# Last two experts added by TensorE, a reworked router chain, and the turns of silu rows between the halves of gate and up, in a one-core transformer layer

## The reference, cut to what matters

```python
h = rms_norm(x, g_attn);  z = h @ w_in            # q, k, v, indexer and gates
o_a, o_b = moba_attention(...), dsa_attention(...)
x = x + (sigmoid(ga) * (o_a @ w_br_a) + sigmoid(gb) * (o_b @ w_br_b)) @ w_out
x = x + hier_moe(rms_norm(x, g_ffn), ...)         # 4 groups of 8 experts
gate = sigmoid(rms_norm(x, g_ple) @ w_ple_gate)
x = x + gate * (p @ w_ple_proj)
return rms_norm(x, g_final)
```

## Time and profile before

| | us |
|---|---|
| median of 3 runs | 1038.18 (1036.38 to 1038.47) |
| the profiled execution | 1035.44 |
| its span | 1033.7 |
| TensorE matmul busy | 957.4 (93%) |
| VectorE, ScalarE, GpSimd busy | 369.2, 306.7, 146.7 |
| expert 0's first product begins | 479.2 |
| last down product ends | 951.1 |
| first turn of a tail tile begins | 965.6 |
| last gate products end | 1023.7 |

### The profile page before, as it was taken

One profiled execution on the slowest core, in us unless ns is written; L12 is line 12 of the kernel. 1 busy time (PEld: TensorE's weight loads), 2 busy tenths in 40 slices (PEclk: granted clock), 3 DMA queues, 4 the chain that ended last, 5 costly groups with the idle time before them and its releaser, 6 DMA issues.

```text
span 1033.7 us, 11751 instructions
## 1 busy us (share of the span) xinstructions
PE 957.4 (93%) x4688; PEld 587.7 (57%) x4688; DVE 369.2 (36%) x760; ACT 306.7 (30%) x527; POOL 146.7 (14%) x143
## 2 busy tenths in 40 slices
PE   5999999999999999987999999999999999997496
PEld 4776787576688888874434444444344334432374
DVE  4325696755453437236121111111011111031764
ACT  6334434746433124142111111111111111212464
POOL 0202123926600000020000000000000000001300
PEclk8999999999999999998999999999999999999698
DMA  9422131000072340846899999999999999999401
GB/s 313 145 82 82 41 114 16 1 2 1 2 285 82 114 171 3 323 158 273 348 420 421 421 421 420 420 421 420 421 422 420 421 421 415 421 420 382 165 21 61
DMA packets 58375, 256.03 MB, mean 248 GB/s; under 512 B 12094, under 2 KB 12734, under 8 KB 33232
## 3 DMA queue, kind: packets, MB, share of 16 engines
q1 hardware_dynamic: 49456, 248.26, 59.9%
q0 software_dynamic: 2560, 4.20, 1.1%
q10 hardware_dynamic: 6304, 2.80, 1.0%
HBM read 248.95 MB, written 10.49 MB: 251 GB/s over the span
## 4 chain that ended last, share of the span: by engine, by line
PE 85%; DVE 5%; DMA 4%; ACT 2%; POOL 2%; issue 1%; SPq 0%; ACTq 0%; POOLq 0%; DVEq 0%
PE psum L678 36%; PE psum L1003 11%; PE psum L1019 10%; PE psum L1004 9%; PE psum L965 6%; DMA slot<-in_w_up 3%; PE psum L984 2%; PE psum L974 2%; PE psum L1037 1%; DVE ht L1773 1%; PE psum L863 1%; PE psum L848 1%; PE psum L836 1%; PE psum L824 1%; DVE ple_gate_lo L1754 1%
## 5 line engine op out<-in xcount | busy, mean ns | idle before, releaser
L1003 PE MATMUL psum<-slot,xt 128*64 128x512 f32 x512 | 226.0, 594 | 2.2 <-DMA slot<-in_w_up 1.6
L1004 PE MATMUL psum<-slot,xt 128*64 128x512 f32 x512 | 226.1, 594 | 0.0
L1019 PE MATMUL psum<-slot,ht 128*64 128x512 f32 x256 | 116.7, 599 | 16.6 <-DVE ht L1773 16.6
L1773 DVE COPY ht<-psum 128x256 f32<-128x256 f32 x32 | 13.6, 425 | 330.7 <-PE psum L984 330.7
L678 PE MATMUL psum<-w_hi,act_hi 128*128 128x512 f32 x288 | 115.2, 400 | 6.1 <-DVE w_lo L544 6.1
L1020 PE MATMUL psum<-slot,ht 128*64 128x512 f32 x256 | 116.7, 598 | 0.0
L678 PE MATMUL psum<-w_lo,act_hi 128*128 128x512 f32 x288 | 112.9, 392 | 0.0
L678 PE MATMUL psum<-w_hi,act_lo 128*128 128x512 f32 x288 | 112.5, 391 | 0.0
L1003 PEld LDWEIGHTS psum<-slot,xt 128*64 128x64 f32 x512 | 68.5, 137 | 77.3 <-issue 75.4
L1004 PEld LDWEIGHTS psum<-slot,xt 128*64 128x64 f32 x512 | 68.5, 137 | 63.5 <-issue 63.4
L544 DVE TENSOR_TENSOR w_lo<-raw,w_hi 128x2048 fp32r<-128x2048 f32 (+1 forms) x31 | 70.5, 2274 | 83.9 <-ACT w_hi L539 83.8
(11 more groups left out here) (266 smaller groups left out, 1413.6 us busy)
## 6 DMA issues: line engine op xcount, KB each, us to landing
slot<-in_w_gate SPq DMA_DIRECT2D x64, 1024.0 KB, 19.0
slot<-in_w_up SPq DMA_DIRECT2D x64, 1024.0 KB, 19.9
slot<-in_w_down SPq DMA_DIRECT2D x64, 1024.0 KB, 20.9
raw<-in_w_in SPq DMA_DIRECT2D x22, 1024.0 KB, 5.0
raw<-in_w_out SPq DMA_DIRECT2D x4, 1024.0 KB, 5.2
slot<-in_w_ple_gate SPq DMA_DIRECT2D x4, 1024.0 KB, 20.9
pair_in<-pair_rows SPq DMA_DIRECT2D x4, 1024.0 KB, 8.3
rows_tok<-in_x SPq DMA_DIRECT2D x4, 512.0 KB, 6.7
```

The source lines that it names most:

```text
L1003: mm_g = pe.matmul(ps[FIRST:2 * FIRST, :], left, g[:, k, :], start=first, stop=last)
L1004: mm_u = pe.matmul(ps[0:FIRST, :], left, u[:, k, :], start=first, stop=last)
L1019: pe.matmul(ps[0:FIRST, :], left, w[:, k, 0:512], start=first, stop=last)
L1773: dve.tensor_copy(ht, h_turns(FIRST)).then_inc(ht_done, 1)
```

## The change

- Router: GpSimd's part of `x1_lo` goes to VectorE (`low_x1`, six pieces); ScalarE does an early Sqrt on a constant and casts tile 2 before it copies its turned rows; logits are four scalar_tensor_tensor instead of two tensor_tensor; the masked logits are one instruction instead of four; the first pick is in two halves, and gather(0) starts on the first.
- TensorE runs 18 products into an unused bank before it waits for the choice of experts, and 3 after the rank (`hold_clock`).
- `turn_hidden(e-1)` moves to between the two halves of `gate_up(e)`.
- Experts 30 and 31 are no longer scattered: `to_token` (the turned pick matrix of each) is made beside experts 28 to 30, `y_hi` and `y_lo` hold the weighed results, and `add_last(t)` multiplies them to token rows in PSUM, which VectorE adds to x. Rows of zeros are scattered at their places after expert 5.
- `pair_in` is read before the last two halves of `w_ple_gate`; GpSimd adds the pairs of all four tiles. The gate weights' splits stand earlier or later, between other steps of the tail. The final gain goes to a slot of its own.
- The regions hi and lo come ahead of the last whi/wlo in the order of slots.

```diff
-SLOT_REGION += [(r, n % SPLIT) for n in range(N_FRONT - SPLIT, N_FRONT) for r in ("whi", "wlo")]
-SLOT_REGION += [("hi", 0), ("lo", 0), ("v", 0), ("rope", 0)]
+NO_ROWS_E = 5
+HOLD = (18, 3)
+SLOT_REGION += [(r, n % SPLIT) for n in range(N_FRONT - SPLIT, N_FRONT - 1) for r in ("whi", "wlo")]
+SLOT_REGION += [("hi", 0), ("lo", 0)] + [(r, (N_FRONT - 1) % SPLIT) for r in ("whi", "wlo")] + [("v", 0), ("rope", 0)]
+X1_LOWS = [(0, None), (1, None), (2, 0), (2, 1), (3, 0), (3, 1)]
...
@@ sync
+        for n, h in enumerate(LOADS[:-2]):
+            load_slot(n, *h)
...
         for t in range(NT):
+            if t == 2:
+                for n in range(len(LOADS) - 2, len(LOADS)):
+                    load_slot(n, *LOADS[n])
+            sp.wait_ge(half_used, PAIR_FREE[t])
             sp.dma_start(pair_in[t]...
@@ tensor
+        def hold_clock(n):
+            for _ in range(n):
+                pe.matmul(bank[4][:, 0:P], ident, c("causal")[:, 0:P], start=True, stop=True)
+
+        hold_clock(HOLD[0])
         pe.wait_ge(halves_made, 2)
         pe.wait_ge(top_done, 1)
...
         mm.then_inc(rank_done, 1)
+        hold_clock(HOLD[1])
...
+        def turn_and_wait(e):
+            pe.wait_ge(hid_done, e + 1)
+            turn_hidden(hid_turned)
@@ gate_up(e)
                 mm_u.then_inc(half_used, 1)
+                if h == 0 and e:
+                    turn_and_wait(e - 1)
@@ the loop over experts
-            pe.wait_ge(hid_done, e + 1)
-            turn_hidden(hid_turned)
+            if e == NE - 1:
+                turn_and_wait(e)
             pe.wait_ge(ht_done, e + 1)
             down(e)
...
+            if e in (NE - 3, NE - 2):
+                n = e - (NE - 3)
+                pe.wait_ge(picked, NE // 2 + 1 + n)
+                pe.wait_ge(xt_done, NE + n)
+                for t in range(NT):
+                    mm = pe.transpose(bank[0][:, t * P:(t + 1) * P], last_pick[:, t, :], ident)
+                mm.then_inc(x_turned, 1)
...
+        def add_last(t):
+            pe.wait_ge(y_done, NE)
+            pe.wait_ge(y_low, 2)
+            pe.wait_ge(xt_done, NE + 2)
             if t >= 2:
                 pe.wait_ge(tail_low, 2 * t - 2)
+            for n in range(4):
+                e, part = n // 2, (y_hi, y_lo)[n % 2]
+                for h in range(2):
+                    at = slice(FIRST * h, FIRST * h + FIRST)
+                    mm = pe.matmul(bank[2 * (t % 2) + h], to_token[at, e, t * P:(t + 1) * P], part[at, e], start=n == 0, stop=n == 3)
...
+        add_last(0)
+        add_last(1)
         turn_tail(0)
         for t in range(NT):
             gate_tail(t, 0)
             if t + 1 < NT:
                 turn_tail(t + 1)
+            if t == 0:
+                add_last(2)
             gate_tail(t, 1)
+            if t == 0:
+                add_last(3)
@@ scalar
+        act.activation(stat[:, 20:21], eps[:], ACT.Sqrt)
...
+            if e == NE - 1:
+                gate_split_high(0)
             weigh(e)
...
-        for m in range(len(PLE_GATE)):
-            gate_split_high(m)
+        gate_split_high(1)
         tail_copy(0)
+        gate_split_high(2)
+        gate_split_high(3)
@@ vector, route()
+            for t in range(NT):
+                ins = dve.scalar_tensor_tensor(out=logits[:, t], in0=bank[0][:, t * (NG + NE):(t + 1) * (NG + NE)],
+                                               scalar=inv_rms[:, t:t + 1], in1=br[:], op0=ALU.mult, op1=ALU.add)
...
+            low_x1(3)
             dve.wait_ge(rank_done, 1)
...
             pick_rows(0)
+            low_x1(4)
+            low_x1(5)
@@ vector, the loop over experts
+            if e == NE - 4:
+                pick_last(0)
+            if e in (NE - 3, NE - 2):
+                dve.wait_ge(x_turned, NE + 1 + e - (NE - 3))
+                dve.tensor_copy(to_token[:, e - (NE - 3)], bank[0]).then_inc(xt_done, 1)
+            if e == NE - 3:
+                pick_last(1)
+            if e == NE - 1:
+                gate_split_low(0)
+            if e >= NE - 2:
+                dve.wait_ge(y_done, e + 1)
+                dve.scalar_tensor_tensor(out=y_lo[:, e % 2], in0=bank[5 + e % 2], scalar=slot_weight[:, e:e + 1],
+                                         in1=y_hi[:, e % 2].bitcast(F32), op0=ALU.mult, op1=ALU.subtract).then_inc(y_low, 1)
@@ vector, tail
-        gate_split_low(0)
+        add_pairs(0)
+        add_last(0)
+        tail_lows(0)
         gate_split_low(1)
-        add_pairs(0)
-        tail_lows(0)
+        add_pairs(1)
+        add_last(1)
         gate_split_low(2)
+        tail_inverse(0)
         gate_split_low(3)
-        add_pairs(1)
-        tail_inverse(0)
         for t in range(NT):
             add_gated(t, 0)
             if t + 1 < NT:
                 tail_lows(t + 1)
             if t == 0:
                 add_pairs(2)
-                add_pairs(3)
+                add_last(2)
+            if t == 1:
+                tail_inverse(2)
             add_gated(t, 1)
             if t == 0:
-                tail_inverse(2)
+                add_pairs(3)
+                add_last(3)
             last_norm(t)
@@ gpsimd
-        for e in range(NE):
+        for e in range(NE - 2):
             pool.wait_ge(y_done, e + 1)
             scatter(slot_pair[:, e:e + 1], y_sb[:, e % 2], scattered[e % 2])
+            if e == NO_ROWS_E:
+                pool.wait_ge(rows_ready, 4)
+                for n in range(2):
+                    scatter(slot_pair[:, NE - 2 + n:NE - 1 + n], no_rows, scattered[n])
...
-        for t in range(1, NT):
+        for t in range(NT):
             pool.wait_ge(x_in[t], 32)
             pool.tensor_tensor(pair_in[t][:, 0], pair_in[t][:, 0], pair_in[t][:, 1], ALU.add).then_inc(pairs_summed, 1)
```

More of the change, by code:

```diff
@@ L281 @@
 PAIR_SLOTS = OVER_SLOTS[:NT]
+PAIR_FREE = [N_USED - len(OVER_SLOTS) + 1 + t for t in range(NT)]
+X1_LOWS = [(0, None), (1, None), (2, 0), (2, 1), (3, 0), (3, 1)]
 X1_TURNS = [("first", 0), ("first", 1), ("first", 2), ("second", 0), ("first", 3), ("second", 1), ("second", 2),
@@ L611, in half_source, with load_slot @@
             return views[what][e][:, h * HALF_W:(h + 1) * HALF_W]
-        for n, (what, e, h) in enumerate(LOADS):
+        def load_slot(n, what, e, h):
             k, need, _ = PLACE[what, e, h]
@@ L1260, in _ @@
         copy_x1("first", 3)
-        for t in (1, 2):
-            square_half(1, t)
-            copy_x1("second", t)
-            high_x1(t)
+        square_half(1, 1)
+        copy_x1("second", 1)
+        high_x1(1)
+        act.activation(stat[:, 20:21], eps[:], ACT.Sqrt)
+        square_half(1, 2)
+        high_x1(2)
+        copy_x1("second", 2)
         square_half(1, 3)
@@ L1612, in route @@
             link(dve.tensor_scalar(pen, group, -1.0, -NEG, ALU.add, ALU.mult))
-            for g in range(NG):
-                ins = dve.tensor_tensor(masked[:, :, g * EPG:(g + 1) * EPG],
-                                        logits[:, :, NG + g * EPG:NG + (g + 1) * EPG],
-                                        pen[:, :, g:g + 1].to_broadcast([P, NT, EPG]), ALU.add)
-            link(ins)
+            by_group = lambda v: v.rearrange("p t (g e) -> p t g e", g=NG)
+            link(dve.tensor_tensor(by_group(masked), by_group(logits[:, :, NG:NG + NE]),
+                                   pen.unsqueeze(3).to_broadcast([P, NT, NG, EPG]), ALU.add))
             marked = block_(3)
@@ L1731, in _ @@
         dve.memset(eps[:], EPS).then_inc(eps_set, 1)
-        dve.memset(table[:], OOB).then_inc(fill_ready, 1)
-        dve.memset(rows[:], 0).then_inc(fill_ready, 1)
+        dve.memset(table[:], OOB).then_inc(rows_ready, 1)
+        dve.memset(rows[:], 0).then_inc(rows_ready, 1)
         for s in FRONT:
@@ L1834, in last_norm, with add_last @@
             dve.wait_ge(gain_in, 2 * 16)
[L1835 removed]
+            dve.scalar_tensor_tensor(out=xres[:, t], in0=xres[:, t], scalar=cols[5], in1=g_last, op0=ALU.mult, op1=ALU.mult
                                      ).then_inc(last_out, 1)
         def add_pairs(t):
[L1839 to L1845 removed]
+            dve.wait_ge(x1_back, NT)
+            dve.wait_ge(pairs_summed, t + 1)
+            link(dve.tensor_tensor(xres[:, t], xres[:, t], pair_in[t][:, 0], ALU.add))
+        def add_last(t):
+            for h in range(2):
+                dve.wait_ge(last_added, 2 * t + h + 1)
+                dst = xres[:, t, h * 512:(h + 1) * 512]
+                ins = dve.tensor_tensor(dst, dst, bank[2 * (t % 2) + h], ALU.add)
+            ins.then_inc(tail_added, 1)
         def tail_inverse(t):
@@ L1911, in _ @@
                 scale_rows(s[1], s[2])
-        for n, (t, a, b) in enumerate(((1, 0, D), (2, 0, D), (3, 0, D // 2))):
-            pool.wait_ge(x1_hi_done, t + 1)
-            pool.wait_ge(x1_turned, X1_TURNS.index(("second", t)) + 1)
-            pool.wait_ge(ssq_done, NT + t + 1)
-            pool.tensor_tensor(x1_lo[:, t, a:b], xres[:, t, a:b], x1_hi[:, t, a:b].bitcast(F32), ALU.subtract).then_inc(x1_lo_pool, 1)
```

(8 more changed lines are left out.)

111 lines of the change are left out of this document (63 added, 48 removed).

## The result

The changed kernel took 1030.43 us (median of 5 runs, 1026.04 to 1033.45), the kernel before beside it 1037.29 (5 runs, 1035.64 to 1038.47): a ratio of 0.9934 with a 95% interval of [0.9922, 0.9946], about 7 us. Run again unaltered in a later comparison it took 1028.51 (1028.12 to 1029.72), ratio 0.9918 [0.9905, 0.9931]. The forecast was 8.1 us and 1030.0. The sum came out; the terms did not: the router and the tail gave less than forecast, the turns more, and these offset one another. The profiled execution of the changed kernel took 1032.11 us, with a span of 1030.3.

What follows compares the result with a forecast made beforehand. The weight stream was taken to bound the experts up to 853 us, then TensorE, with latency and VectorE in the tail. 7.0 + 1.1 = 8.1 us, 3.0 the router's, the rest the tail's, gave 1030 from 1038.18; range 1021.5 to 1035.5.

Steps and rivals of the forecast that it cites:

- (a): Router chain on VectorE: faster 128x4 add and freed sums 1.9 us, logits 0.8, masked add 0.2; choice 2.9 us sooner.
- (b): Router: 18 held products bridge 4.3 us, gather falls from 5.71 to about 3.75; VectorE has 1.35 us more before in_row.
- (c): Router's end: VectorE, not TensorE, is late next; expert 0 starts 3.0 us sooner, bounds 1.0 and 5.2.
- R4: Rival: held products delay the rank by 2.9, or gate_up starts at the slow level; router gains 0 to 1; 15%.
- (d): Experts: turns remove up to 16 us of waits, worth nothing up to 853; end 1.2 us sooner, outside the sum.
- R1: Rival: TensorE, not DMA, bounds the experts and nearly all 16 us of the turns come: 1018; 5%.
- (e): Last two experts by TensorE without scatter: tail tile ready at 957.3 instead of 965.6, 8.3 us gained.
- (f): Tail: VectorE sets the pace, each GpSimd sum costs 2.1; gate_tail(1,0) at 980.3, 7.0 us sooner, plus 1.1 of stall.
- A -3.0, B -5.3, C +0.2: Stretches: A, copy x1t to gate_up(0)'s end; B, to first tail turn; C, to ScalarE's start on the last gate product.
- R2: Rival: VectorE is not in the way of xt (5.2) and the tail's low parts are not slowed: 1025; 20%.
- R3: Rival, slower: everything new in the tail lands in series, +0.8 to +3.4 us: 1040; 5%.

Runs made afterwards that it cites:

- router alone: The kernel before with only the router's part of the change, slot order, turns and tail left as before: 1035.92 us, 0.9984.
- changed, again: The changed kernel run and profiled again, no edit, in a later comparison: 1028.51 us, 0.9918 to the kernel before.
- turns back: The changed kernel with the silu rows' turns put back behind the next expert's gate_up: 1031.56 us, 0.9948 to the kernel before.
- pairs on VectorE: The changed kernel with the sums of pair_in 2 and 3 on VectorE instead of GpSimd: 1028.41 us, 0.9918 to the kernel before.

## Why the prediction was right, and where it was not

(a) Right in the main. The add fell to 0.15, GpSimd silent; the masked add to 0.29. The logits took 0.74, not 0.55, since four 36-wide instructions are 0.19 apart. The choice of experts was ready 2.7 us sooner, counted from the copy x1t, not 2.9.

(b) Right. The held products took 4.26 us (4.3), the gather with the full level ran from 468.95 to 472.85, 3.9 us where 3.75 was worked out. Taking them all away changed nothing that the comparison shows.

(c) Right in its size at the point where it was put: xt 3.0 us sooner in the changed kernel and with the router alone, and expert 0 began 3.0 sooner. What failed is the step after it, that the 3.0 are kept in full. The text had the lower bound, 1.0, "if TensorE, idle for 2.9 us before gate_up, runs it at the slow level", and gave it to R4. The idle time was 2.0, and of five traces with it (changed, again, turns back, router alone, pairs on VectorE) four had four to seven pairs at the slow level, one of them only from the third pair on; none of the other eight, which waited 0.83 or less. The router was worth 1.7 [0.7 to 2.6], not 3.0: the second half of R4, gate_up at the slow level, came in four of five traces, where R4 as a whole was given 15%.

(d) The mechanism was right, shown twice: with 16 us of waits taken from TensorE, its waits for weights grow by 10.5 and 10.8, R1 is refuted, and in the kernel before the edit is worth nothing. The end of the experts was wrong. The last down product was to come at 946.9, and came at 952.49 and 949.52. Counted from the end of gate_up(0) it was to be 1.2 us sooner than before and was 1.1 later, in both profiles. By single traces the turns took 3.3 off (against turns put back), where 3.0 were booked; the router's part alone added 2.5, where none was, by waits for weights; the rest added 1.9, where 1.8 were booked. The miss cost nothing in these two profiles, because pair_in 0 was last. The 1.2 us were put outside the sum; in the changed kernel the comparison gives the turns 1.4 to 3.1 us, the trace 0.3 in B. That gap is not settled.

(e) The mis-sized term. The first turn of a tail tile was to come at 957.5. It came at 962.26 in the first profile, past the 962 that the prediction named as a sign of being wrong, and at 959.29 in the second, with gate_up(0) at full level; that level makes the whole difference between the two. The chain was the forecast one: pair_in 0 last, behind the gate loads, and its add slowed by the second sum, which the prediction had booked (953.1 to 956.0, 2.9 us). Only sizes were off. From the end of gate_up(0), forecast for 483.3, pair_in 0 was to land 467.4 us later and landed 468.2 later in both profiles. VectorE's add ended 3.5 us behind the first sum instead of 2.9, of which 0.5 is idle before it. The two make 1.4 of the 1.6 us missing in B. B fell by 3.7 us, where 965.6 to 957.3 less the router's 3.0 would have been 5.3. The prediction gave no working for the landing at 950.7; the gate load at 945.7 and two more megabytes of 2.5 us give it, and that gate load itself landed 0.7 later than forecast, counted the same way.

(f) Right in price, wrong in the picture. Two sums beside VectorE were to cost 4.2 in low part 1 and the add of pair 1. In the second profile they did, 2.1 and 2.2 (4.87 for 2.73, 3.41 for 1.21); in the first the low parts paid all of it and the add of pair 1, with no sum beside it, took 1.21. The 1.8 on the add of pair 0 had been booked in (e). But the low pieces, forecast at 1.2 us each beside GpSimd, took either 0.74 or, one per sum, 2.8 to 2.9. The rule from the Trainium skill that was weighed there (GPSIMD Engine Reference, Specifications: VectorE suffers with two SBUF inputs or in a two-port mode) agrees with the traces as to which instructions are held: y_lo, with an input from PSUM, took 0.74 us beside a sum as without one, while an add or a low part with two SBUF inputs, begun beside a running sum, ended 1.1 or 0.55 us behind it. The products of gate_tail(1, 0) came at 985.67 and 982.07, not 980.3, by what (c) and (e) lost. The stall of 1.1 us for tail_lows(2) is gone.

The forecast had A -3.0, B -5.3, C +0.2. The two profiles of the changed kernel have A -0.1 and -3.0, B -3.7 in both, C 0 and -0.6. By differences of the ratios (before 1037 us) the router gives 1.7 us, the turns 1.4 to 3.1 and the tail, from router alone to turns put back, 3.7; the new order of the slots, booked at nothing, is in that share. The forecast was 3.0, 0 and 5.1. So the total was right with too much for the first and third part, and too little for the second; that these offset one another is luck.

R2 needed VectorE out of the way of xt and the low parts not slowed, and neither came. R3, slower because all in series, did not come. Its point of decision, y_lo behind the gate load, was real, and the kernel with pair_in 0 on the other queue ran into it.

## What to carry to other kernels

When a stage is fed by a saturated queue, taking away an engine's waits is no gain by itself: ask which wait comes in their place, and for a transfer on the path count what is queued ahead of it, not its own length (here four loads of 1 MB, landing about 2.6 us apart). When a stretch is shortened so that TensorE idles before a heavy stage, look at the clock behind the idle time; giving it its input one instruction sooner (a step of VectorE moved ahead of an independent one, 3 us by the comparison, of which 1.2 are this mechanism) was worth more than keeping it busy with held products. Where VectorE sets the pace with SBUF operands, moving work to GpSimd to relieve it can do the opposite: each sum of 1.2 us taken back onto VectorE freed 2.1 on its path.

## What the runs showed of the hardware

- VectorE and GpSimd took turns. From the router on, in all thirteen traces, an instruction of VectorE with two SBUF inputs that began while a GpSimd add or subtract ran ended a fixed time behind it: twenty low parts (0.74 us by themselves) 0.55 or 0.56 us behind, six 128x1024 adds (1.22) 1.08 or 1.09, the 128x4 add (0.15) 0.02, however long they had waited (1.6 to 2.9 us for a low part, 2.7 to 3.4 for an add). Where VectorE's add began 0.01 to 0.2 us ahead of the sum, in three traces, it kept its 1.2 us and the sum took 3.3 to 3.4 instead of 2.35. Instructions with an input from PSUM (y_lo 0.74) kept their length.
- The clock after a short idle time. After 2.0 us without products TensorE began gate_up(0) at the full level in one trace and fell to the 1.2 GHz level in four, three times from the first pair and once from the third. The same 16 pairs took 7.0 us in one trace of the changed kernel and 9.9 in the other, and 8.7 in the three others.
- The lag of the last part of a weight half. Each weight half lands in sixteen parts, and the trace has the landing of each. Worked out from these records for the kernel before, the last part came 0.1 us behind the median one at 515 us, and 2.4 to 2.8 behind it from 875 to 925 us; over all thirteen traces it was 0.1 to 2.0 and 1.9 to 3.5. The lag grew in jumps, and the lasting jumps of 0.7 us or more (at 526, 744 and 860 us in the kernel before) came 2 to 4 us after the start of a 16 KB transfer of instructions (the page's queue q8, one about every 26 us), in all thirteen traces. The last of them came in the kernel before behind the landing of the up half of expert 26 (852.9), and in the changed kernel at 826, ahead of it (856.4). The lag of that half was 1.0 us before and 2.6 then, about 1.5 of the 3.1 us by which it landed later against the end of gate_up(0). It was seen in the traces and not tested by a run.
- A full queue seems to hold back its issuer: in the trace of before SyncE's issues of two down halves took 0.8 us at 497 us and 5.8 at 843. A slot given back sooner then only lengthens the queue; that last step is argued, not tested.
